# A two-block transformer kernel on one Trainium2 core: row sums for the modulation vectors, query norm in the exponential's scale, late expert queries between gather slots

## What is computed

```python
def ada_mod(c, w, b):                      # 4 times, w: (1024, 3072)
    m = jax.nn.silu(c) @ w + b
    shift, scale, gate = jnp.split(m, 3, axis=-1)
    return shift[:, None, :], 1.0 + scale[:, None, :], 1.0 + gate[:, None, :]

def dsa_attention(...):                    # first attention
    q = rope(rms_norm(q.reshape(B, T, 16, 64), q_gain), cos, sin)
    ...
    s = jnp.einsum('qgrd,qkgd->qgrk', q_blk, k_sel) * 64 ** -0.5
    p = jax.nn.softmax(jnp.where(valid, s, -jnp.inf), axis=-1)

def chunk(xc):                             # the experts, 128 tokens
    q = (xc @ w_q).reshape(128, 8, 2, 128)
    s = jnp.einsum('thpd,pnd->thpn', q, sub_keys)
    ... # top 16 of 16 x 16 candidates: idx, and g = softmax(top_s)
    act = jax.nn.gelu(jnp.einsum('td,thkd->thk', xc, u[idx]))
    return jnp.einsum('thk,thkd->td', g * act, v[idx])
```

## Time and profile before

| | us |
|---|---|
| median of 3 runs | 2483.12 |
| lowest, highest | 2474.12, 2490.23 |
| the profiled execution | 2481.21 |
| its span, first to last instruction | 2479.4 |

### The profile page before, as it was taken

One profiled execution on the slowest core, in us unless ns is written; L12 is line 12 of the kernel. 1 busy time (PEld: TensorE's weight loads), 2 busy tenths in 40 slices (PEclk: granted clock), 3 DMA queues, 4 the chain that ended last, 5 costly groups with the idle time before them and its releaser, 6 DMA issues.

```text
span 2479.4 us, 28805 instructions
## 1 busy us (share of the span) xinstructions
PE 2148.4 (87%) x9964; PEld 1390.4 (56%) x9964; DVE 1605.8 (65%) x3630; ACT 1132.3 (46%) x2756; POOL 639.6 (26%) x624
## 2 busy tenths in 40 slices
PE   7768999997999998887887898897898898888876
PEld 7647999876999997732322443442344443233322
DVE  5785676647676755667666657646738756676753
ACT  4343543534453343344444547434539534444543
POOL 0000001001001001544444334334324334444441
PEclk8768999998999998999999999999999999999998
DMA  5223568434557753799999999999999999999995
GB/s 213 86 94 127 171 227 301 152 134 155 187 187 280 253 172 102 273 409 421 421 421 422 395 416 400 398 418 422 401 418 378 416 386 407 421 421 422 421 422 216
DMA packets 138871, 767.74 MB, mean 310 GB/s; under 512 B 15216, under 2 KB 18032, under 8 KB 72944
## 3 DMA queue, kind: packets, MB, share of 16 engines
q0 software_dynamic: 87552, 587.24, 58.5%
q1 hardware_dynamic: 50464, 177.29, 20.4%
q10 hardware_dynamic: 720, 1.51, 0.2%
HBM read 764.93 MB, written 1.05 MB: 309 GB/s over the span
## 4 chain that ended last, share of the span: by engine, by line
PE 52%; DMA 25%; DVE 12%; ACT 7%; issue 3%; POOL 1%; SPq 0%; ACTq 0%; DVEq 0%; POOLq 0%
DMA arena<-experts,arena 23%; PE bank L865 13%; PE bank L507 9%; PE bank L509 9%; PE bank L508 9%; PE bank L900 6%; DVE arena L2076 3%; DMA wring<-w_stream 2%; DVE arena L1614 1%; ACT L1334 1%; ACT arena L1339 1%; PE bank L648 1%; POOL arena L473 1%; DVE arena L1663 1%; ACT arena L1338 1%
## 5 line engine op out<-in xcount | busy, mean ns | idle before, releaser
L865 PE MATMUL bank<-arena 128*128 128x512 f32 x2048 | 986.0, 619 | 165.3 <-ACT arena L1339 165.2
L2076 DVE CUSTOM_DVE_ANT_0 arena<-arena 128x1024 f32<-128x1024 f32 x512 | 626.1, 1224 | 468.5 <-DMA arena<-experts,arena 467.7
L865 PEld LDWEIGHTS bank<-arena 128*128 128x128 f32 x2048 | 373.3, 194 | 731.7 <-ACT arena L1339 382.7
L473 POOL DMA_INDIRECT arena<-experts,arena x512 | 560.0, 1094 | 865.2 <-PE bank L865 822.2
L1560 DVE TENSOR_TENSOR wlo<-wring,whi 128x1024 fp32r<-128x1024 f32 x224 | 272.9, 1224 | 195.8 <-ACT whi L1089 194.8
L507 PE MATMUL bank<-hTh,whi 128*128 128x256 f32 (+1 forms) x1152 | 340.8, 296 | 31.7 <-DVE hTl L1569 24.6
L1089 ACT CAST whi<-wring 128x1024 fp32r<-128x1024 f32 x236 | 245.9, 1047 | 206.2 <-PE bank L509 204.6
L509 PE MATMUL bank<-hTh,wlo 128*128 128x256 f32 (+1 forms) x1152 | 335.4, 291 | 0.0
L508 PE MATMUL bank<-hTl,whi 128*128 128x256 f32 (+1 forms) x1152 | 335.1, 291 | 0.0
L1334 ACT ACTIVATE arena<-arena 128x1 f32<-128x1 f32 x512 | 103.1, 201 | 482.8 <-DVE arena L2076 481.1
L507 PEld LDWEIGHTS bank<-hTh,whi 128*128 128x128 f32 x1152 | 225.3, 196 | 40.8 <-issue 30.6
(11 more groups left out here) (289 smaller groups left out, 2537.0 us busy)
## 6 DMA issues: line engine op xcount, KB each, us to landing
wring<-w_stream SPq DMA_DIRECT2D x332, 512.0 KB, 4.3
alibi<-ada_w POOLq DMA_DIRECT2D x64, 512.0 KB, 5.1
arena<-ada_w POOLq DMA_DIRECT2D x32, 512.0 KB, 4.8
arena<-experts,arena POOLq DMA_INDIRECT x512, 14.6
xT<-xT_in SPq DMA_DIRECT2D x1, 1088.0 KB, 5.2
alibi<-alibi_in ACTq DMA_DIRECT2D x1, 1024.0 KB, 7.5
outT<-xT SPq DMA_DIRECT2D x2, 512.0 KB, 13.5
tab<-tab_in SPq DMA_DIRECT2D x1, 831.0 KB, 7.0
```

The lines of the kernel that those rows point to most:

```text
L473: pool.indirect_dma_start(g_ring[:, r], None, experts[n // (2 * PEER_HEADS)], bass.IndirectOffsetOnAxis(idx[:, s // SLOTS % 2, s % SLOTS:s ...
L865: last = mm(banks[2 * t + b][:, :], diag[:, r], g_ring[:, r, D + b * TILE_N:D + (b + 1) * TILE_N], start=s % SLOTS == 0, stop=s % SLOTS == ...
L2076: v.tensor_tensor_reduce(g_ring[:, r, 0:D], g_ring[:, r, 0:D], hrow[:, t], 1.0, 0.0, ALU.mult, ALU.add, act8[:, r:r + 1]).then_inc(dot_don ...
```

## The change

Three edits, and what follows from them.

*Row sums.* `ada_w` is laid out the other way round: a block is 128 output features by 1024 input features. silu(c) is loaded as a row repeated on all partitions (`c_in`, 512 KB, on SP behind the gate weights), and `ada_part` becomes one product with row sum on VectorE that writes one column of `adaM`. `ada_reduce` and its four places on TensorE go, with the waits on them. The ring of three lies beside the row and no longer in `alibi`. The second attention has no steps any more: six of its 18 stand between the last key and query scalings before it, twelve beside the convolution's low parts.

*Query norm.* The four query pairs aren't divided by their norm. VectorE multiplies gain and rotary table in one step (`rope_query`, no root awaited); `pair_sums` makes sums with tokens on partitions, 6 small matmuls for a pair, the roots go to `q_root`, and one reciprocal and one product make `q_scale`, which is the exponential's per-row scale and a factor of the negative maximum. The key pair stays as it was.

*Slots.* `BESIDE_HEAD` becomes (0, 0, 0, 10, 14, 14, 14, 0): 52 slots before the last scores. `gate_exp(0)` moves to step 3, gates 1 and on follow their slots' order (`coefficient`, `tick`). POOL makes one more low part before the first gather, three between the first six, and the last four behind gathers 12, 14, 22 and 24.

```diff
     return parts_due(s) - (parts_due(s - 1) if s % SLOTS else 0)
-BESIDE_HEAD = (0, 0, 0, 0, 0, 1, 2, 2)
-EARLY = sum(BESIDE_HEAD)
+BESIDE_HEAD = (0, 0, 0, 10, 14, 14, 14, 0)
+LOW_BESIDE = {12: 0, 14: 1, 22: 2, 24: 3}
 ROWS = [(0, N_META), (N_META, P), (N_META + P, P)]
...
         first = carve(0)
-        ada_acc = first(2, 3, D)
-        ada_ring = [first(D), *(alibi[:, 4 * x:4 * x + 4].rearrange("p a q -> p (a q)") for x in range(2))]
+        c_row = first(D)
+        ada_ring = [first(D) for _ in range(3)]
         FIRST = first.at[0]
...
                 split_lo(G_PQ + 1, c)
+            split_lo(G_PQ + 2, 0)
             pool.wait_ge(hrow_done, 4)
-            for s in range(RING):
+            for s in range(N_SLOTS):
                 gather(s)
-                if s % 2:
-                    split_lo(G_PQ + 2, s // 2)
-            for c in range(CPT):
-                split_lo(G_PQ + 3, c)
-            for s in range(RING, N_SLOTS):
-                gather(s)
+                if s in (1, 3, 5):
+                    split_lo(G_PQ + 2, (s + 1) // 2)
+                elif s in LOW_BESIDE:
+                    split_lo(G_PQ + 3, LOW_BESIDE[s])
...
                         chunk(g, c, banks[c][:, 0:n], rhs)
-            def ada_reduce(b):
-                pe.wait_ge(ada_used, 24 * (b + 1))
-                if b:
-                    pe.wait_ge(ada_ready, b)
-                for n in range(24):
-                    last = mm(banks[5][:, n:n + 1], ada_acc[:, b % 2, n // 8, n % 8 * P:(n % 8 + 1) * P],
-                              ones[:, 0:1], start=True, stop=True)
-                last.then_inc(ada_red, 1)
             def mlp(layer, n0):
...
                     pe.wait_ge(pair_rt, n - 1)
-                mm(banks[4 + n % 2][:, 0:T], table("block32"), sq_pair[:, n % 2, 0], start=True, stop=False)
-                mm(banks[4 + n % 2][:, 0:T], table("block32"), sq_pair[:, n % 2, 1], start=False,
-                   stop=True).then_inc(pair_ss, 1)
+                if n == 0:
+                    for half in range(2):
+                        last = mm(banks[4][:, 0:T], table("block32"), sq_pair[:, 0, half], start=half == 0, stop=half == 1)
+                else:
+                    heads = table("block32").rearrange("p (b c) -> p b c", b=4)[:, :, 0]
+                    for r, (q0, nq) in enumerate(ROWS):
+                        for half in range(2):
+                            last = mm(banks[4 + n % 2][0:nq, 4 * r:4 * r + 4], sq_pair[:, n % 2, half, q0:q0 + nq], heads,
+                                      start=half == 0, stop=half == 1)
+                last.then_inc(pair_ss, 1)
             pair_sums(0)
...
                             af(att_p[layer][0:nq, n % 3, b, 0:w], att_sm[layer][0:nq, n % 2, b, 0:w], ACT.Exp,
-                               scale=HD ** -0.5 if layer == 0 else 1.0, bias=att_nmx[0:nq, n % 2, b:b + 1],
+                               scale=1.0 if layer else q_scale[0:nq, r, 4 * x + b:4 * x + b + 1], bias=att_nmx[0:nq, n % 2, b:b + 1],
                                accum_out=att_sum[0:nq, n % 2, b:b + 1]).then_inc(exp_done, 1)
...
                 af(sq_pair[:, n % 2, 1], banks[b + 1][:, 0:T], ACT.Square).then_inc(pair_sq, 1)
-            def pair_root(n, w, scale, eps):
+            def pair_root(n):
                 act.wait_ge(pair_ss, n + 1)
-                if n >= 2:
-                    act.wait_ge(pair_done, n - 1)
-                af(rt[:, n % 2, 0:w], banks[4 + n % 2][:, 0:w], ACT.Sqrt, scale=scale,
-                   bias=vcol("eps", eps)).then_inc(pair_rt, 1)
+                if n == 0:
+                    af(rt[:, 0], banks[4][:, 0:T], ACT.Sqrt, scale=1.0 / HD, bias=vcol("eps", 0)).then_inc(pair_rt, 1)
+                    return
+                h = slice(4 * (n - 1), 4 * n)
+                af(q_root[0:N_META, 0, h], banks[4 + n % 2][0:N_META, 0:4], ACT.Sqrt, scale=1.0 / HD, bias=vcol("eps", 0)[0:N_META])
+                af(q_root[:, 1:3, h], banks[4 + n % 2][:, 4:12].rearrange("p (r b) -> p r b", r=2), ACT.Sqrt, scale=1.0 / HD,
+                   bias=vcol("eps", 0)).then_inc(pair_rt, 1)
             pair_squares(0, G_KV, 0, 0)
...
             hi_parts(hTh, hf, 0, SEQ, mod_ready, mod_hi, 8)
+            def coefficient(s):
+                gelu(s)
+                if s % PK == 2 and s < (TURNS - 1) * PK:
+                    gate_exp(s // PK + 1)
+                if s == LAM_AT:
+                    act.wait_ge(lam_sum, 1)
+                    af(lexp, lsum, ACT.Exp).then_inc(lam_exp, 1)
             early = 0
...
                         nc.scalar.copy(hrow[:, t, b * TILE_N:(b + 1) * TILE_N], banks[b][:, :]).then_inc(hrow_copied, 1)
-                if h == 5:
+                if h == 3:
                     gate_exp(0)
                 for _ in range(BESIDE_HEAD[h - 1] if h else 0):
-                    gelu(early)
+                    coefficient(early)
                     early += 1
-            gate_exp(1)
             act.wait_ge(sk_done, PEER_HEADS)
...
                 ada_at[0] += 1
-                b, kc, third = n // 24, n // 3 % KC, n % 3
-                acc, w = ada_acc[:, b % 2, third], c_silu[:, kc:kc + 1]
                 dve.wait_ge(ada_landed[n % 3], 16 * (n // 3 + 1))
-                if kc == 0:
-                    if b >= 2:
-                        dve.wait_ge(ada_red, b - 1)
-                    v.tensor_scalar(acc, ada_ring[n % 3], w, None, ALU.mult).then_inc(ada_used, 1)
-                else:
-                    dve.wait_ge(ada_used, n - 2)
-                    v.scalar_tensor_tensor(acc, ada_ring[n % 3], w, acc, ALU.mult, ALU.add).then_inc(ada_used, 1)
+                v.tensor_tensor_reduce(ada_ring[n % 3], ada_ring[n % 3], c_row, 1.0, 0.0, ALU.mult, ALU.add,
+                                       adaM[:, n // 24, n % 24:n % 24 + 1]).then_inc(ada_used, 1)
             def residual(g0, n0, last_of_tile, beside):
...
                 N = N_QUADS[layer]
-                parts = ((0, 0, 0, 0, 1, 1, 1, 2, 2, 2, 2, 0, 0, 0, 0), (2, 2, 2, 2, 2, 2, 2, 2, 2, 0, 0))[layer]
+                parts = ((0, 0, 0, 0, 1, 1, 1, 2, 2, 2, 2, 0, 0, 0, 0), (0, 0, 0, 0, 0, 0, 0, 0, 0, 0, 0))[layer]
                 def masked(n):
...
                     dve.wait_ge(sm_done, 4 * at + 4)
-                    v.tensor_scalar(att_nmx[0:nq, n % 2], att_mx[0:nq, n % 2],
-                                    -(HD ** -0.5) if layer == 0 else -1.0, None, ALU.mult).then_inc(nmx_done, 1)
+                    if layer:
+                        v.tensor_scalar(att_nmx[0:nq, n % 2], att_mx[0:nq, n % 2], -1.0, None, ALU.mult).then_inc(nmx_done, 1)
+                    else:
+                        v.scalar_tensor_tensor(att_nmx[0:nq, n % 2], att_mx[0:nq, n % 2], -1.0, q_scale[0:nq, r, 4 * x:4 * x + 4],
+                                               ALU.mult, ALU.mult).then_inc(nmx_done, 1)
                 def turned(n):
...
                 rope(pairn[:, 0], pairn[:, 1], out_a, out_b, pair_done)
+                dve.wait_ge(pair_done, n + 1)
+            def rope_query(n):
+                b, x = Q_BANK[n - 1], n - 1
+                dve.wait_ge(pair_sq, n + 1)
+                for t, (half, turn) in enumerate(((0, "cos"), (1, "sin"), (0, "sin"), (1, "cos"))):
+                    mark(v.scalar_tensor_tensor(rope_t[:, t], banks[b + half][:, 0:T], vcol("gain_q", half), table(turn),
+                                                ALU.mult, ALU.mult))
+                settle()
+                mark(v.tensor_tensor(qA[:, 2 * x], rope_t[:, 0], rope_t[:, 1], ALU.subtract))
+                v.tensor_tensor(qA[:, 2 * x + 1], rope_t[:, 2], rope_t[:, 3], ALU.add).then_inc(pair_done, 1)
                 dve.wait_ge(pair_done, n + 1)
...
                     split_lo(4, 2 * n - 1)
-                pair_norm(n, Q_BANK[n - 1], "gain_q", qA[:, 2 * n - 2], qA[:, 2 * n - 1])
+                rope_query(n)
                 if n == 2:
...
             dve.wait_ge(silu_done, 1)
+            dve.wait_ge(pair_rt, 5)
+            link(v.reciprocal(q_scale, q_root))
+            link(v.tensor_scalar(q_scale, q_scale, HD ** -0.5, None, ALU.mult))
             attention(0)
...
                 head_scale(8 + x)
+                ada_part()
             split_lo(G_BV + 2, 0)
...
                 head_scale(8 + x)
+                ada_part()
             split_lo(G_BV + 2, 2)
             split_lo(G_BV + 2, 3)
+            ada_part()
             attention(1)
...
             for g in range(G_CONV + 1, G_CONV + 5):
-                split_los(g)
+                for c in range(CPT):
+                    split_lo(g, c)
+                    if c:
+                        ada_part()
+            ada_add(3)
             dve.wait_ge(conv_copied, 16)
...
                     lo_part(zcl[:, c], zcT[:, c], zch[:, c], zc_hi, c + 1, zc_split)
-            ada_add(3)
             dve.wait_ge(ada_ready, 4)
...
             for n in range(TURNS):
-                if n == 1:
-                    gate_norm(1)
```

52 lines of the change are left out of this document (20 added, 32 removed).

## The result

| | before | after |
|---|---|---|
| median of the runs, us | 2484.01 (4 runs, 2474.12 to 2490.23) | 2451.09 (4 runs, 2445.68 to 2453.5) |
| profiled execution, us | 2481.21 | 2449.92 |
| its span, us | 2479.4 | 2448.1 |
| first gather of expert rows, us | 1001.42 | 974.49 |

The ratio is 0.9873, with an interval from 0.9843 to 0.9904: 1.3% faster, 31.3 us between the two profiled spans. The forecast was 2441, which is 43 us less than the median of before in this table (its own sum was 40.8), with a range from 2424 to 2458.

What follows compares the result with a forecast made beforehand. Bound: TensorE, VectorE and ScalarE by turns until about 1000 us, full DMA engines from about 1050. Terms 14 + 10.0 + 2.3 + 2.0 + 7.5 + 6.7 - 1.0 - 0.7 = 40.8 us off 2481.21; forecast 2441, range 2424 to 2458.

Steps and rivals of the forecast that it cites:

- query norm, to the first masks: Before the first attention: cheaper query pairs on VectorE let the masks begin at 123.6, not 130.30; 6.7 us, bounds 4 to 9.
- first attention: dearer sums, scale: First attention: two exposed row sums cost 1.0 us more, the exponential's scale read from memory 0.7 us more.
- first set: 24 column products dropped from TensorE ahead of the keys, taken as a place like the second set's; 2.0 us.
- second attention: Its 18 modulation steps go; the fifth block begins at 570.0, not 575.5; 7.5 us in sum, bounds -1 to 21.
- third set: 24 column products dropped mid second MLP, TensorE-bound: 7.82 us plus 2.2 for the low clock behind; 10.0 us.
- fourth set: Dropping these column products gains nothing: behind them TensorE still waits for VectorE's convolution chain; 0 us.
- gathers' start: Earlier expert slots fill the hole in the DMA stream from 1030 to 1060 us; 14 us, bounds 0 to 15.
- ninth gather: TensorE takes slot 0 at about 1021, so this gather leaves at about 1024 and joins a stream still running.
- rival B: Second attention is VectorE's if ScalarE's loop shrinks too: 21 us instead of 7.5, total 2427 us; chance 0.12.
- rival A: Late GpSimd low parts each hold VectorE 2.4 us; early gathers' gain falls to 0 to 5, total 2450 to 2455; chance 0.24.
- Rival C: TensorE's clock stays low among the 52 early slots, costing 49 us; total 2490 us; chance 0.02.
- D: Column products partly hidden: sum loses 2.2, or 6.5 with the other two sets, total 2447; chance 0.58 with the forecast.

Runs made afterwards that it cites:

- e3: Kernel before with only the new order of gathers, low parts and queries; 2474.4 us, ratio 0.9962.
- e4: Kernel before with one of the 24 column products in each of the four sets on TensorE; 2466.61 us, ratio 0.9939.
- e2: Changed kernel with the order of gathers, low parts and queries of before; 2463.65 us, ratio 0.9938.
- e7: Changed kernel with 64 bytes per partition of padding, putting the gathered rows' ring at its address of before; 2446.47 us, ratio 0.986.
- e8: Kernel before with the new 512 KB input added, eight columns of it loaded and nothing used; 2482.27 us, ratio 0.9997.
- e6: Changed kernel with 24 extra matmuls on TensorE between the first and second block's scores of the second attention; 2449.56 us, ratio 0.9876.
- e5: Changed kernel with the four late low parts on VectorE, behind products 12, 14, 28 and 30, not on GpSimd; 2453.36 us, ratio 0.989.
- e11: Changed kernel with 224 bytes of padding, putting the gathered rows' ring at a multiple of 512 bytes; 2431.6 us, ratio 0.9806.

## Why the prediction was right, step by step

The time lay in the range and the sign was right; 33 us came where the sum had 40.8. By the terms of the sum, in the profiled run:

| term | forecast, us | measured, us | read at |
|---|---|---|---|
| the start, 0 to 92 us | 0 | 3.4 | first mark; the execution's (e3) |
| query norm, to the first masks | 6.7 | 8.0 | masks at 118.94 against 130.30, less 3.4 |
| first attention: dearer sums, scale | -1.7 | 0.0 | second mark, 11.4; 0 to 2.8 between executions |
| behind it, to 246 us | 0 | 1.1 | 0.5 to 1.1 with the change, 0 to 0.4 with the code of before |
| first set | 2.0 | 0.0 | third mark, and e4 |
| second attention | 7.5 | 2.8 | fourth mark; 4.7 in e2, e7 |
| second set | 2.3 | 1.8 | 2.3 in e4 |
| third set | 10.0 | 10.1 | fifth and sixth mark, 9.9 in e4; 6.9 against e8 |
| fourth set | 0 | 0.2 | lies ahead of the set, at 857 us; at the set 0.0, -0.4 in e4 |
| selection | 0 | -0.5 | 27.4 behind the fourth set, 26.9 at the gather |
| gathers' start | 14 | 11.3 | gather 80; 11.0 in e7, 11.9 in e3 |
| the stream behind it, tail | 0 | -6.9 | some 4 to 5 the ring's place (e2, e6, e7), the rest single losses |
| sum | 40.8 | 31.3 | |

Three steps held. *The third set* came out at 10.1 for 10.0, price and clock both; that it fits to 0.1 is luck in part, for in e8 the same set cost 3.2 us less, by its clock. *The fourth* was covered, as said, though by other cover: TensorE now waits 8.0 us there for the convolution's low parts (3.84, 2.97, 0.72 and 0.45), where the row of before has 0.45. Two of the four waits, in the timeline of TensorE in the changed kernel:

```profile
898.51 0.55 PE L509 MATMUL bank<-zch,whi 128*128 128x256 f32 x1 [3.84 <-DVE zcl L1565]
...
902.45 0.58 PE L509 MATMUL bank<-zch,whi 128*128 128x256 f32 x1 [2.97 <-DVE zcl L1565]
```

*The ninth gather* left 21.7 us behind the first for the 22.6 that the path was worked out at. The total owes something to luck: terms that were too high (the second attention, the gathers' start, the first set) and a loss that was not in the sum (the stream) stand against terms that were too low and 3.4 us of start that are the execution's.

"The first set, at the same kind of place ahead of the keys, I put at 2.0 us by this row": this failed. It is not the same kind of place. Behind the norm's sums VectorE has sixteen pieces to make there, and the chain that ended last runs through them for 14 us. The chain of before, where TensorE's products stood on it, and then the changed kernel's, from its norm on:

```profile
438.99 6.22 PE bank L648 x48
```

```profile
427.06 1.86 DVE rinv L1570
...
437.15 0.35 DVE hTl L1565
...
440.57 0.40 ACT arena L1274
```

TensorE is released by ScalarE at 440.97; the products lay wholly beside this, and with one product in place of 24 (e4) the lead did not change here either.

"I laid out the first four blocks with VectorE's pieces and ScalarE's": in the second attention this missed the engine that took over. Between the first masks and 561 us the chain now runs through TensorE without a gap: 15.1 us from 546.29 on, up to 558.8 of it at half clock. At full clock the same scores take about half (0.76 against 1.33 to 1.55 for eight). Of the 5.5 us forecast for the first blocks 1.5 came here, 3.5 in e2. The later blocks kept their 6.56 us (561.40 to 567.96) and gave 1.2 with the tail, where 2.0 were forecast, so rival B was rightly held small; but its opposite, a TensorE at half clock, was no rival for this stage. The earlier trace rows had shown what the clock does, and in the profile of before it was at 0.50 from 563 to 568 us too.

The query norm gave 1.3 us more than its 6.7, and 7.9 to 8.0 in every run with the change. The first masks on VectorE and the last pair's square on ScalarE in the changed kernel, which answer to the earlier trace rows:

```profile
118.94 0.16 DVE L1653 CUSTOM_DVE_ANT_0 arena<-bank,tab 16x16 f32<-16x16 f32 x1
```

```profile
110.24 0.40 ACT L1222 ACTIVATE arena<-bank 128x272 f32<-128x272 f32 x1 [2.50 <-PE bank L511]
```

"The last pair can start at about 116 and not at 113": this was too late. The rotation of a pair no longer waits for its sums, so the last one started at 111.10, 0.5 us behind the last square (110.24 + 0.40). With the 3.4 us of the start added that is 114.5. The six small matmuls cost 0.37 us per pair (7.33 us a pair against 6.96), not 1.0. The scale pointer is as forecast. Groups of ScalarE by form, the exponential of 272 columns before and after:

```profile
L1154 ACT ACTIVATE arena<-arena 128x272 f32<-128x272 f32 x16 | 8.1, 510 | 9.0 <-DVE arena L1666 9.0
```

```profile
L1144 ACT ACTIVATE arena<-arena 128x272 f32<-128x272 f32 x16 | 9.6, 602 | 7.6 <-DVE arena L1659 7.6
```

That is 92 ns for the 87 of the earlier trace rows. What the first attention feels of it can't be told well: from the first masks to the second mark of the ladder it is 76.7 us, and 75.4 to 77.3 in the other runs with the change; with the code of before it is 76.8 in three profiles and 74.0 in e3 and e4. The shortest with the change is 1.4 us longer than the shortest without, for the 1.7 forecast.

The gathers' start gave 11.3 of 14. The missing 3 us are rival A's mechanism (e5: 3.5 to 3.8 us), with about the price per part that it named, 2.5 to 2.9 for 2.4. It was right about the place and wrong about the size: the ring didn't run dry for good. TensorE's pause was 9.2 us (1017.94 to 1027.17) and not 7 to 8, which by e5 cost nothing. The Trainium skill (SBUF — State Buffer, Who interferes with whom) says that VectorE and GpSimd share one pair of ports under an exclusive lock, that a VectorE instruction with two SBUF inputs contends with a GpSimd instruction that reads SBUF, and that a cast can contend too, in the modes that use both ports. The traces agree that they exclude each other: the product at 1010.35 ends 1.1 us, about its own length, behind GpSimd's part, and a cast of 32 elements took 3.03 us at 1004.59, to 0.05 us behind the end of one. In both it is VectorE's that is late, and GpSimd's keeps its 2.35 us.

Rival C didn't come: among the early slots the clock is 1.00, 0.83, 1.00, 1.00 and 0.85 in the five stretches shown at the top, and 0.71 in the one before them (990 to 1000). D fell with e4 for the second and the third set, and held for the first alone.

And the forecast had nothing for the stream's own speed. "The bytes moved are the same, so a gather begun earlier moves everything behind it" is true of bytes and not of time: dropping 64 bytes of small tensors cost 0.3 to 0.4% of the stream (420 for 421 GB/s, 400.7 for 399.1 us).

## What to carry to other kernels

Where a stream fills the DMA engines, try the address of its SBUF buffer: the same kernel took 2451, 2446 or 2432 us with 0, 64 or 224 bytes of padding ahead of it, the last at a multiple of 512, and an edit that only drops a small tensor can move it. Three places were tried, no more. Where a side engine's work moves beside VectorE's, price it by what it holds up there: 2.5 us and more of VectorE's time, where VectorE does the same part itself in 1.2. And when forecasting a stage from which one engine's load is taken, lay out all the engines at the clock that the stage really had, TensorE included.

## What the runs showed that was not expected

- The ring's address. Where it lies 288, 352 and 0 bytes behind a multiple of 512 by the program's layout (the changed kernel, before and e7, e11), the stream runs at 420, 421 and 427 GB/s, and 161 gathers take 400.7, 399.1 and 394.3 us. The Trainium skill (DMA: Bandwidth & Descriptors, How a descriptor splits into AXI transactions) says that a descriptor which doesn't start at a multiple of 256 bytes has its first transaction begin at the boundary below and pays for the surplus. The runs agree on the aligned place (1.4% faster than the next). The rule does not explain why 96 bytes past such a boundary (352) is better than 32 (288), and no run tells a multiple of 256 from one of 512.
- Executions of the same code differ by 3 us in the first 92 us, by 2 to 3 us in each attention and by 3 us at the third set, with the granted clock at one or the other of its levels for some microseconds more. Marks inside the profile separate this from the change where medians of some runs, 2474 to 2490 for the kernel before, can't.
- In every run with the change TensorE was at half clock for 6.9 us or more of the second attention's first half. The longest such stretch, 13.7 us, cost 2 us over the shortest, and matmuls that filled the wait ahead of it only moved the fall (e6).
